# Order of logits, of the normed rows' transposes and of their splits in the output stage

## The reference

```python
h = rms_norm(x, mix_norm_g)
u_a, v_a, q, k, v = split(h @ w_in)
y_a = spatial_gating(u_a, v_a, ...)
y_b = window_sink_attention(q, k, v, sinks, rel_bias)   # 64-row chunks, window of 128 keys
x = x + concat(rms_norm(y_a), rms_norm(y_b)) @ w_out
h = rms_norm(x, ffn_norm_g)
x = x + (silu(h @ w_gate) * (h @ w_up)) @ w_down
out = rms_norm(x, final_norm_g)
```

## Time and profile before

| | us |
|---|---|
| median of 3 executions | 932.45 (931.69 to 932.66) |
| the profiled execution: its span | 930.2 |
| TensorE busy (matmuls) | 921.3 (99%) |
| VectorE busy | 551.3 (59%) |
| ScalarE busy | 403.6 (43%) |
| GpSimd busy | 329.1 (35%) |

### The profile page before, as it was taken

The page is one execution under the profiler, slowest core; times in us unless marked ns, Lnnn a source line. Parts: engine busy times, 40 slices in busy tenths (PEclk is TensorE's granted clock), DMA queues, the critical chain, the costliest instruction groups (busy, mean ns, idle before and its releaser), DMA issues.

```text
span 930.2 us, 11930 instructions
## 1 busy us (share of the span) xinstructions
PE 921.3 (99%) x4277; PEld 757.5 (81%) x4277; DVE 551.3 (59%) x812; ACT 403.6 (43%) x833; POOL 329.1 (35%) x344
## 2 busy tenths in 40 slices
PE   9999999999999999999999999999999999999997
PEld 7888888878778878888888888888888888888885
DVE  5655773576677966564553645537446676544753
ACT  6743541465655733333333323333335355434451
POOL 1410000022125288575674765755753100000022
PEclk9999999999999999999999999999999999999999
DMA  9621312312224334726437365273557897656643
GB/s 337 229 79 57 89 41 88 88 46 87 73 98 130 102 114 158 226 77 218 153 108 227 99 195 179 90 241 90 182 179 259 317 394 230 188 198 194 191 138 133
DMA packets 132000, 147.02 MB, mean 158 GB/s; under 512 B 16281, under 2 KB 92645, under 8 KB 131941
## 3 DMA queue, kind: packets, MB, share of 16 engines
q1 hardware_dynamic: 131268, 145.86, 48.3%
q10 hardware_dynamic: 672, 0.40, 0.1%
HBM read 105.73 MB, written 40.50 MB: 157 GB/s over the span
## 4 chain that ended last, share of the span: by engine, by line
PE 94%; issue 2%; DVE 2%; DMA 1%; ACT 0%; POOL 0%; DVEq 0%; POOLq 0%; ACTq 0%
PE ps L703 30%; PE ps L705 29%; PE ps L704 29%; PE ps L830 1%; PE ps L849 1%; PE ps L907 1%; PE ps L840 1%; PE ps L779 1%; DMA A22s<-in_w_gate 1%; DVE P_lo L1703 0%; DMA small<-in_mix_gT 0%; DVE T_lo L1690 0%; PE ps L733 0%; PE ps L736 0%; PE ps L739 0%
## 5 line engine op out<-in xcount | busy, mean ns | idle before, releaser
L1703 DVE TENSOR_TENSOR P_lo<-P_raw,P_hi 128x512 fp32r<-128x512 f32 x132 | 118.1, 910 | 82.5 <-ACT P_hi L1227 75.2
L703 PE MATMUL ps<-T_hi,P_hi 128*128 128x512 f32 x352 | 137.1, 389 | 0.0
L705 PE MATMUL ps<-T_hi,P_lo 128*128 128x512 f32 x352 | 136.9, 389 | 0.0
L704 PE MATMUL ps<-T_lo,P_hi 128*128 128x512 f32 x352 | 136.9, 389 | 0.0
L703 PE MATMUL ps<-rb_hi,ra_hi 128*128 128x512 f32 x308 | 119.8, 389 | 0.0
L704 PE MATMUL ps<-rb_lo,ra_hi 128*128 128x512 f32 x308 | 119.8, 389 | 0.0
L705 PE MATMUL ps<-rb_hi,ra_lo 128*128 128x512 f32 x308 | 119.8, 389 | 0.0
L647 POOL TENSOR_TENSOR wd<-wd 128x256 f32<-128x256 f32 x88 | 82.9, 942 | 95.0 <-DMA wd<-in_w_down 89.9
L1328 ACT ACTIVATE ra_hi<-ra 128x512 fp32r<-128x512 f32 x77 | 48.6, 632 | 98.3 <-DMA rb<-w_down_T 58.1
L1783 DVE TENSOR_TENSOR ra_lo<-ra,ra_hi 128x512 fp32r<-128x512 f32 x77 | 56.2, 730 | 37.6 <-ACT ra_hi L1328 37.3
L1227 ACT ACTIVATE P_hi<-P_raw 128x512 fp32r<-128x512 f32 x132 | 76.6, 620 | 3.5 <-POOL P_raw L607 3.5
(11 more groups left out here) (208 smaller groups left out, 1911.4 us busy)
## 6 DMA issues: line engine op xcount, KB each, us to landing
wd<-in_w_down SPq DMA_DIRECT2D x44, 256.0 KB, 3.3
w_down_T<-wd SPq DMA_DIRECT2D x22, 512.0 KB, 5.0
ra<-act_S SPq DMA_DIRECT2D x44, 256.0 KB, 2.7
rb<-w_down_T SPq DMA_DIRECT2D x44, 256.0 KB, 3.0
act_S<-Q SPq DMA_DIRECT2D x33, 256.0 KB, 3.7
ra<-act_A SPq DMA_DIRECT2D x33, 256.0 KB, 5.0
rb<-in_w_down SPq DMA_DIRECT2D x33, 256.0 KB, 5.9
P_raw<-in_w_gate SPq DMA_DIRECT2D x22, 256.0 KB, 3.7
```

Of the source, the lines that this page charges most:

```text
L703: mm(dst, lhs[0], rhs[0], start=start, stop=False, skip_group_check=onto)
L704: mm(dst, lhs[0], rhs[1], start=False, stop=False, skip_group_check=onto)
L705: return mm(dst, lhs[1], rhs[0], start=False, stop=stop, skip_group_check=onto)
L1703: tt(w_l[p, m][:], src[:], w_h[p, m][:].bitcast(F32), ALU.subtract).then_inc(w_split, 1)
```

## The change

Three orders are changed, on TensorE, ScalarE and VectorE. On TensorE `logits(r+2)`, which stood ahead of `out_unit(r+1, 1)`, becomes `logits(r+3)` behind `values(r+1)`, in r = 0 too; `h2_transposed(r-1, 0)` goes from ahead of `out_unit(r+1, 1)` to behind the logits, and `h2_transposed(r-1, 1)` from behind `values(r+1)` to behind `out_unit(r, 3)`, both for r = 1 to T - 3 = 5. On ScalarE `h2_split(r-1, 0)` goes behind the exponentials, to where its second half was, and the second half to the head of the next iteration. On VectorE `h2_lo(r-1, 0)` goes behind `normal_probs(r+2)`, and the second half to the head of the next iteration. Row T - 2 = 6 keeps its own order. The waits themselves are unchanged.

```diff
--- before.py
+++ after.py
@@ -920,23 +920,23 @@
                     out_unit(r + 1, 0)
                     probs_T(r + 1, 1)
                     yb_rows(r)
-                if 0 < r < T - 2:
-                    logits(r + 2)
                 if r + 1 < T:
-                    if 0 < r < T - 2:
-                        h2_transposed(r - 1, 0)
                     out_unit(r + 1, 1)
                     if r == T - 2:
                         h2_transposed(r - 1, 0)
                     values(r + 1)
+                    if r + 3 < T:
+                        logits(r + 3)
                     if 0 < r < T - 2:
-                        h2_transposed(r - 1, 1)
+                        h2_transposed(r - 1, 0)
                 out_unit(r, 2)
                 if r == T - 2:
                     h2_transposed(r - 1, 1)
                 if r == T - 2:
                     yb_rows(r + 1)
                 out_unit(r, 3)
+                if 0 < r < T - 2:
+                    h2_transposed(r - 1, 1)
 
             def product(i, p, m):
                 pe.wait_ge(w_split, split_at(i, p, m))
@@ -1239,6 +1239,8 @@
             woB_piece(2)
 
             for r in range(T):
+                if 1 < r < T - 1:
+                    h2_split(r - 2, 1)
                 if r + 1 < T:
                     probs_to_sbuf(r + 1, 0)
                 if r == 0:
@@ -1247,7 +1249,7 @@
                     x2_square(r - 1)
                 if r + 1 < T:
                     probs_to_sbuf(r + 1, 1)
-                    if r:
+                    if r == T - 2:
                         h2_split(r - 1, 0)
                 exps = probabilities(r + 2) if r + 2 < T else None
                 if exps:
@@ -1256,7 +1258,9 @@
                     yb_to_sbuf(r + 1)
                 if exps:
                     next(exps)
-                if r and r + 1 < T:
+                if 0 < r < T - 2:
+                    h2_split(r - 1, 0)
+                if r == T - 2:
                     h2_split(r - 1, 1)
                 if r + 2 < T:
                     yb_square(r + 1)
@@ -1718,6 +1722,8 @@
             add_out(1, 0)
             woB_piece(1)
             for r in range(T):
+                if 1 < r < T - 1:
+                    h2_lo(r - 2, 1)
                 if r:
                     norm_x2(r - 1)
                 if r and r + 1 < T:
@@ -1731,14 +1737,16 @@
                     woB_piece(2)
                     woB_piece(3)
                 if r + 1 < T:
-                    if r:
+                    if r == T - 2:
                         h2_lo(r - 1, 0)
                     add_out(r + 1, 1)
                     yb_lo(r + 1)
                 add_out(r, 2)
                 if r + 2 < T:
                     normal_probs(r + 2)
-                if r and r + 1 < T:
+                if 0 < r < T - 2:
+                    h2_lo(r - 1, 0)
+                if r == T - 2:
                     h2_lo(r - 1, 1)
                 add_out(r, 3)
                 if r == T - 2:
```

## The result

The changed kernel takes 937.05 us (median, 936.62 to 939.19) against 932.45: ratio 1.0055, 95% interval 1.0043 to 1.0067, 4.6 us slower. The forecast was 936.2, 3.8 slower.

The account below looks back on a forecast made before the run. TensorE, busy 99% of the span, was taken to bound the kernel. Start 211.11 plus four rounds of 15.94 gave 274.87, so probs_T(7, 0) at 275.33, 3.76 us later: 932.45 + 3.76 = 936.2 us, range 934.0 to 938.2.

Parts of the forecast that it names:

- The wait: TensorE idle before h2_transposed(r-1, 1) until h2_lo(r-1, 0) ends: 0.45 us first, 0.82 a row, 1.91 in r=5; 4.8 in all.
- the round: Closed chain from late transposes via split, norm_x2, exponentials, normalization and h2_lo back: 15.94 us a row, over TensorE's 15.12.
- the 3.17 us path: From out_unit(r, 2)'s end over add_out, denominators, normalization and h2_lo to TensorE: 3.17 us against out_unit(r, 3)'s 2.72, costing 0.45.
- The hand-overs: Passing from ScalarE's last exponential to VectorE, and from h2_lo to TensorE: 0.06 us each in the round.
- the start: First late transposes, h2_transposed(0, 1), start at 211.11 us, with TensorE free for them at 210.66.
- TensorE's groups: Work between output units: 0.93 us for eight transposes, 0.58 for probs_T and yb_rows, 2.73 for values, logits, h2_transposed; row 15.12.
- the values-to-logits seam: TensorE's switch from values to logits matmuls, not in the trace: bounded by 0.15 us either way, taken as none.
- (B): Rival: ScalarE takes the late split off the round; rows 15.57 us apart, 934.1 us (+1.7); chance 0.09.
- (C): Rival: bank 7 wait not met, since h2_lo ends before out_unit(r, 3) does; 931.4 us, 1.1 earlier; chance 0.06.
- (D): Rival: GpSimd's halving sum starts before VectorE's normalization in every row, adding five times 0.38 us: 938.1; chance 0.08.
- The tail: Rows 6 and 7, from probs_T(7, 0) on: TensorE works without a gap, so nothing gives the 3.76 us delay back.

Follow-up runs that it names:

- probs_first: Changed kernel with h2_transposed(r-1, 1) behind probs_T(r+2, 0) instead of ahead of it on TensorE: 936.77 us, ratio 1.0049 to the kernel before.
- both: Changed kernel with late transposes behind probs_T, and their split and h2_lo behind the second pT copy and the maxima: 932.95 us, ratio 1.0008.
- split_late: Changed kernel with the late half's split behind the second pT copy on ScalarE and its h2_lo behind the maxima on VectorE: 936.36 us, ratio 1.0044.
- logits_alone: Kernel before with only the logits moved, logits(r+3) behind values(r+1): 938.43 us, ratio 1.0067.
- late_half_alone: Kernel before with only h2_transposed(r-1, 1), its split and its h2_lo moved to the places of the change: 933.25 us, ratio 1.0013.
- after_longer_split2: Changed kernel with one more ScalarE copy in the late half's split: 940.33 us, ratio 1.0088 to the kernel before.

## Why the prediction came out

**Direction and mechanism: right.** The wait stands where it was placed, before `h2_transposed(r-1, 1)`, released by `h2_lo(r-1, 0)`, in all five rows, and the rows follow the round's length. `probs_first` shows that it isn't the 3.17 us path beside `out_unit(r, 3)`, and the longer split that the split is a link: 1.91 us for four copies of 0.49. `both` shows that the grouping on TensorE costs nothing that can be told.

**Size: 0.85 us too small, from three terms.** (1) The hand-overs: I took 0.06 for each from one case; in the round they are 0.10 (ScalarE to VectorE) and 0.15 (VectorE's `h2_lo` to TensorE), 0.13 a round, so 16.07 for 15.94. Over four rounds this is 0.52; the start comes at 211.24 for 211.11, by its own hand-over out of `h2_lo` (0.09) and TensorE free at 210.69 for 210.66, so 0.65 together. (2) The first round is 16.43. In it `norm_x2` starts at 215.88 [above], 0.46 us behind GpSimd's root, in the others 0.10 behind. The root:

```profile
214.87 0.55 POOL L561 TENSOR_TENSOR late<-late,small 128x1 f32<-128x1 f32 x1
```

It ends at 214.87 + 0.55 = 215.42. The kernel before has the same delay in the same row (in its timeline the root ends at 213.40, `norm_x2` starts at 213.86), where it cost nothing; I took the link from r = 4 only. What it is, no run shows: it stands at this row in nine of the eleven traces, and is 0.11 in `split_late` and `both`. That is 0.36. (3) A little comes back: the end moved by 4.7, `probs_T(7, 0)` by 4.77, and the medians by 4.6, since the changed kernel's lies 2.15 above its profiled span and not 2.25. Together 276.34 for the predicted 275.33, and 5.6 us of waits for 4.8.

**TensorE's groups: right.** 2.74 for 2.73, 0.60 for 0.58, no wait before the logits, the values-to-logits seam within its bound.

**The rivals.** (B), rows 15.57 apart, is refuted by 16.07; and when the split was taken off the round in `split_late`, the rows were 15.98 and not 15.57, for B had left out the next wait on the bank. (C) would need rows without waits; all five have one. (D) isn't in the changed kernel: the normalization takes 1.22 to 1.23 us there in every row from r = 1 on, and GpSimd's sum begins behind its start. But what it rests on is real: it is what `logits_alone` and `late_half_alone` met. The Trainium skill, SBUF — State Buffer, section "Who interferes with whom", has a VectorE instruction with two SBUF inputs blocked by a GpSimd instruction that started first, for the whole of it; the ends at 244.35 and 244.33 agree. The loss is a little less than what was left of the sum: 0.68 - 0.16 = 0.52 of 0.66 us there, 0.56 of 0.72 in `late_half_alone`, and 0.38 of 0.53 in the kernel before.

**The tail: right.** r = 6 and 7 and the products gave back less than 0.1 us.

## What to carry to other kernels

Before work is put off behind other work, list who waits for the resource it frees: here one PSUM bank is handed from transpose to copy to subtraction to transpose, and the deferred subtraction became the gate of the engine that bounds the kernel. If the chain so made leads back to itself a row later, its sum of links, not any single wait, is the row's time, and covering the wait on the waiting engine buys nothing. Follow every reader of what a moved step makes later or frees later: `split_late` and `late_half_alone` came out slower than I expected because I had missed a second one. And where a shift in time changes which of GpSimd and VectorE starts first, look for what that does, as in `logits_alone`.

## What the runs showed of the hardware

In `after_longer_split2` TensorE issued nothing from 275.12 to 277.83; behind that its granted clock fell (0.54 in the mean of 3.7 us), and its work took 1.6 us longer. Behind the changed kernel's 1.87 us of idleness it did not fall.

An 8-column VectorE operation of 0.16 us took 0.68 in `logits_alone` behind a GpSimd sum that had begun 0.08 us earlier, and a 1024-column one of 1.23 took 1.79 in `late_half_alone` behind one that had begun 0.02 earlier.

Hand-overs between engines in this stage differ by their ends: 0.06 us from the normalization to the transposes of its result (kernel before, r = 5), and in the changed kernel 0.10 from ScalarE's exponential to VectorE and 0.15 from `h2_lo` to the transposes into its bank.
